# Down products of a feed-forward block copied by ScalarE and added to the residual by an accumulating transfer, with three operand turns moved back to TensorE

## The reference

```
h = h + jnp.concatenate([oa, ob, oc, od], axis=-1) @ w_out[i]
y = _rms(h, norm_ffn_g[i])
h = h + (jax.nn.silu(y @ w_gate[i]) * (y @ w_up[i])) @ w_down[i]
y = _rms(h, norm_ple_g[i])
h = h + jax.nn.sigmoid(y @ w_ple_gate[i]) * (p[i] @ w_ple_proj[i])
return _rms(h, final_norm_g)
```

## Time and profile before

| | us |
|---|---|
| median of three runs | 2066.68 (2064.77 to 2067.17) |
| the profiled execution, its own time | 2066.98 |
| its span, first to last instruction | 2065.2 |
| PE busy in the span | 2039.0 |
| DVE busy | 1583.2 |
| ACT busy | 1041.8 |
| POOL busy | 175.6 |
| mean granted clock of TensorE, share of full speed | 0.996 |

### The profile page before, as it was taken

How to read it: one execution, slowest core, us unless ns; L and a number is a source line. 1 busy time by engine, 2 the same in 40 slices (tenths; PEclk the granted TensorE clock), 3 DMA queues, 4 the chain that set the end, 5 groups by cost and what they waited for, 6 DMA issues and landing times.

```text
span 2065.2 us, 24990 instructions
## 1 busy us (share of the span) xinstructions
PE 2039.0 (99%) x10231; PEld 1733.1 (84%) x10231; DVE 1583.2 (77%) x1511; ACT 1041.8 (50%) x979; POOL 175.6 (9%) x354
## 2 busy tenths in 40 slices
PE   9999999999999999999999998999999999999998
PEld 8888888888888888888999987888888888888787
DVE  6576565665688888856889868989888889888565
ACT  6444444544455555645344445554555545455543
POOL 2000110010000000023000012111110011110100
PEclk9999999999999999999999999999999999999999
DMA  8655556555465655666655566765666665566561
GB/s 251 215 183 177 180 171 190 172 189 194 166 224 204 224 204 183 204 233 205 206 186 165 178 220 199 234 213 194 198 214 224 214 212 194 194 232 224 173 207 58
DMA packets 234689, 408.33 MB, mean 198 GB/s; under 512 B 16226, under 2 KB 61530, under 8 KB 234320
## 3 DMA queue, kind: packets, MB, share of 16 engines
q1 hardware_dynamic: 221344, 387.64, 56.7%
q0 software_dynamic: 12480, 17.98, 3.1%
q10 hardware_dynamic: 752, 1.12, 0.2%
HBM read 394.62 MB, written 2.12 MB: 192 GB/s over the span
## 4 chain that ended last, share of the span: by engine, by line
PE 87%; DVE 9%; ACT 1%; DMA 1%; issue 1%; POOL 1%; ACTq 0%; SPq 0%; DVEq 0%
PE psA L750 20%; PE psA L752 20%; PE psA L751 20%; PE psA L957 6%; PE psB L750 5%; PE psB L751 5%; PE psB L752 5%; PE psA L961 3%; DVE lo L1759 3%; DVE CA L2083 1%; POOL squares in X L679 1%; DVE raw L1776 1%; DMA squares in X<-squares in X 1%; DVE lo in Y L1759 1%; ACT hi L1274 0%
## 5 line engine op out<-in xcount | busy, mean ns | idle before, releaser
L1759 DVE TENSOR_TENSOR lo<-raw,hi 128x2048 fp32r<-128x2048 f32 (+2 forms) x364 | 822.3, 2268 | 254.1 <-ACT hi L1274 253.0
L1274 ACT ACTIVATE hi<-raw 128x2048 fp32r<-128x2048 f32 (+2 forms) x364 | 688.9, 1899 | 469.8 <-PE psA L752 303.9
L750 PE MATMUL psA<-hi,XHL 128*128 128x512 f32 x1008 | 394.1, 391 | 0.8 <-DVE XHL L1860 0.8
L752 PE MATMUL psA<-hi,XHL 128*128 128x512 f32 x1008 | 391.0, 388 | 0.0
L751 PE MATMUL psA<-lo,XHL 128*128 128x512 f32 (+1 forms) x872 | 338.0, 388 | 0.0
L750 PE MATMUL psA<-hi,YHL 128*128 128x512 f32 x624 | 244.3, 391 | 0.0
L752 PE MATMUL psA<-hi,YHL 128*128 128x512 f32 x624 | 243.3, 390 | 0.0
L750 PEld LDWEIGHTS psA<-hi,XHL 128*128 128x128 f32 x1008 | 189.6, 188 | 40.0 <-issue 1.5
L752 PEld LDWEIGHTS psA<-hi,XHL 128*128 128x128 f32 x1008 | 189.4, 188 | 39.1
L751 PE MATMUL psA<-lo,YHL 128*128 128x512 f32 x536 | 209.1, 390 | 0.0
L751 PEld LDWEIGHTS psA<-lo,XHL 128*128 128x128 f32 x872 | 164.2, 188 | 32.6
(11 more groups left out here) (441 smaller groups left out, 3003.7 us busy)
## 6 DMA issues: line engine op xcount, KB each, us to landing
raw<-in_w_in_dram SPq DMA_DIRECT2D x149, 1024.0 KB, 5.1
raw<-in_w_up_dram SPq DMA_DIRECT2D x35, 1024.0 KB, 5.2
raw<-in_w_gate_dram SPq DMA_DIRECT2D x35, 1024.0 KB, 5.2
raw<-in_w_out_dram SPq DMA_DIRECT2D x32, 1024.0 KB, 5.1
raw<-in_w_down_dram SPq DMA_DIRECT2D x32, 1024.0 KB, 5.2
raw<-in_w_ple_gate_dram SPq DMA_DIRECT2D x14, 1024.0 KB, 5.1
raw<-in_w_branch_dram SPq DMA_DIRECT2D x13, 1024.0 KB, 5.1
raw in Y<-in_w_down_dram SPq DMA_DIRECT2D x12, 1024.0 KB, 5.1
```

The costliest lines, as they stand in the source:

```text
L750: e.matmul(dst, A2[0], B2[0], start=first, stop=False, skip_group_check=True)
L752: return e.matmul(dst, A2[1], B2[0], start=False, stop=last, skip_group_check=True)
L1274: e.activation(hi[u % H][:, 0:m], raw[slot][:, 0:m], ACT.Copy).then_inc(hi_made, 1)
L1759: e.tensor_tensor(lo[slot][:, 0:m], raw[slot][:, 0:m], hi[u % H][:, 0:m].bitcast(F32), ALU.subtract).then_inc(lo_made, 1)
```

## The change

The residual sums of the first nine down parts (36 products) leave VectorE. ScalarE copies each from PSUM into a new tile TD (which takes the place of HB), and GpSimd issues a DMA that adds TD to 512 columns of X (`accum_op=ALU.add`). The copy waits until the sum before it has landed (`x_added`), and GpSimd's DMA waits for the copy. The four products of the last down part stay with VectorE. The hidden block is now written over CG, its squares are moved into THF, and so two waits are new: ScalarE's copy of unit x waits for the squares of the hidden block before, and its first tanh waits until the moved block has been read. The moved block is read at unit BEGIN[j + 1] + 2 (6 for j = 0), and before at + 8. Three turns of X (FIRST 2, SECOND 2, THIRD 0; 24 transposes) go from the second way to the first, and the units at which TensorE turns X are set anew. The iterations of the row scale of the feed-forward norm go from VectorE to GpSimd, 14 steps with a wait behind each. GpSimd's queue in the feed-forward part holds, for each turn: eight DMAs of the move, the sum of down product 0, eight DMAs of the move, the sums of products 1, 2 and 3.

```diff
-        self.by_act = kind != "T2" and name[0] in ("narrow", "qi", "v", "gate", "v2", "scc", "proj", "ple")
+        self.by_act = kind != "T2" and (name[0] in ("narrow", "qi", "v", "gate", "v2", "scc", "proj", "ple")
+                                        or name[0] == "down" and name[1] < 4 * LAST_TURN)
...
-            HB = sb("HB", [128, 2, 512], F32, p4)
+            TD = sb("TD", [128, 1024], F32, p4)
...
+        def emptied(name):
+
+            g = named[name]
+            return bank_act if g.by_act else bank_dve, g.freed
...
-        MOVES = (0, 1, 2, FIRST, FIRST + 1, FIRST + 2, SECOND, SECOND + 2) + tuple(HIDDEN + j for j in range(10)) + (THIRD,)
+        MOVES = (0, 1, 2, FIRST, FIRST + 1, SECOND) + tuple(HIDDEN + j for j in range(10))
...
-        TURN1 = {OUT + 18: 3}
-        TURN2 = {OUT2 + 10: 1, OUT2 + 18: 3}
+        TURN1 = {OUT + 6 + 4 * f: f for f in (2, 3)}
+        TURN2 = {OUT2 + 6 + 4 * f: f for f in (1, 2, 3)}
...
-        TURN3 = {named["down", LAST_DOWN + f].last + 5 - f: f for f in (1, 2, 3)}
-        MOVEDX = {OUT + 8: (FIRST, 0, 16), OUT + 12: (FIRST, 1, 16), OUT + 15: (FIRST, 2, 16),
-                  OUT2 + 8: (SECOND, 0, 32), OUT2 + 15: (SECOND, 2, 32), named["down", LAST_DOWN].last + 5: (THIRD, 0, 48)}
+        TURN3 = {named["down", LAST_DOWN + f].last + 2: f for f in range(4)}
+        MOVEDX = {OUT + 8: (FIRST, 0, 16), OUT + 12: (FIRST, 1, 16), OUT2 + 8: (SECOND, 0, 32)}
...
-        MOVEDH = {BEGIN[j + 1] + 8: j for j in range(10)}
+        MOVEDH = {BEGIN[j + 1] + (2 if j else 6): j for j in range(10)}
...
+            def ffn_root():
+
+                y, w = rr_, w2_
+                e.wait_ge(root_begun, 1)
+                for _ in range(3):
+                    finish(e.tensor_tensor(w, y, y, ALU.mult))
+                    finish(e.tensor_tensor(w, w, v2, ALU.mult))
+                    finish(e.tensor_scalar(w, w, -0.5, 1.5, ALU.mult, ALU.add))
+                    finish(e.tensor_tensor(y, w, y, ALU.mult))
+                finish(e.tensor_scalar(hr2, y, 0.5, None, ALU.mult))
+                e.tensor_tensor(r2h, hr2, y, ALU.mult).then_inc(ffn_scales, 1)
...
-            for j in range(10):
-                move(HIDDEN + j, turning(block_of(j)), flat(HB[:, :, :]))
-            move_x(THIRD, 0)
+            ffn_root()
+            def add_down(n):
+
+                f = n % 4
+                e.wait_ge(*emptied(("down", n)))
+                e.dma_start(cols(f), TD[:, :].rearrange("p (t n) -> p t n", t=2), accum_op=ALU.add).then_inc(x_added, 16)
+
+            move(HIDDEN, turning(block_of(0)), THF[:, :])
+            for j in range(9):
+                n, squares = HIDDEN + j + 1, turning(block_of(j + 1))
+                move(n, squares, THF[:, :], (0, 1))
+                add_down(4 * j)
+                move(n, squares, THF[:, :], (2, 3))
+                for f in (1, 2, 3):
+                    add_down(4 * j + f)
...
                     elif j:
-                        e.wait_ge(*up(j - 1, "hidden"))
+                        e.wait_ge(squares_turned, squared(HIDDEN + j - 1))
                     e.activation(gates_sum[:, 512:1024], quarter(g, "C"), ACT.Copy).then_inc(sum_copied, 1)
...
                     e.wait_ge(ffn_scales, 1)
+                    if j:
+                        e.wait_ge(flip_low, HIDDEN + j)
                     e.activation(THF[:, 512:1024], CG2, ACT.Tanh, scale=hr2[:, 1:2])
...
-                elif name == "down" and n >= LAST_DOWN:
+                elif name == "down" and n < LAST_DOWN:
+                    if n:
+                        e.wait_ge(x_added, 16 * n)
+                    take(TD[:, :])
+                elif name == "down":
                     e.wait_ge(bank_dve, g.freed)
                     squares(n - LAST_DOWN, X, ss4, ss4_made)
...
-                elif name == "down":
+                elif name == "down" and n >= LAST_DOWN:
                     f = n % 4
+                    e.wait_ge(x_added, 16 * LAST_DOWN)
                     e.wait_ge(unit_done, g.last + 1)
                     e.wait_ge(bank_dve, g.freed - 1)
                     e.tensor_tensor(cols(f), cols(f), ps.rearrange("p (t n) -> p t n", t=2), ALU.add).then_inc(bank_dve, 1)
-                    if n == LAST_DOWN:
-                        e.wait_ge(bank_dve, g.freed)
-                        turn_x_squares(f)
```

More of the change, by code:

```diff
@@ L410, in build_hybrid @@
         bank_act, bank_dve, crossed = sem("bank_act"), sem("bank_dve"), sem("crossed")
-        act_step, dve_step = sem("act_step"), sem("dve_step")
+        act_step, dve_step, pool_step, root_begun = [sem(n) for n in ("act_step", "dve_step", "pool_step", "root_begun")]
         x_landed = [sem(f"x_landed{i}") for i in range(4)]
@@ L447, in build_hybrid @@
         squares_turned, squares_moved = sem("squares_turned"), [sem(f"squares_moved{i}") for i in range(2)]
+        x_added = sem("x_added")
         sum_copied, gate_made, up_made, gates_ready = [sem(n) for n in ("sum_copied", "gate_made", "up_made", "gates_ready")]
@@ L672, in gpsimd_program, with finish, move @@
         def gpsimd_program(e):
-            def move(n, squares, dst):
+            steps = [0]
+            def finish(x):
+                steps[0] += 1
+                x.then_inc(pool_step, 1)
+                e.wait_ge(pool_step, steps[0])
+            def ffn_root():
[8 more added lines that the diff above has]
+                e.tensor_tensor(r2h, hr2, y, ALU.mult).then_inc(ffn_scales, 1)
+            def move(n, squares, dst, quads=range(4)):
                 to = dst.rearrange("p (q n) -> p q n", q=4)
                 e.wait_ge(squares_turned, squared(n))
-                for q in range(4):
+                for q in quads:
                     for r in range(4):
@@ L716, in gpsimd_program @@
                     e.dma_start(FW[:, :], rows(A["final_norm_w"], 2048)).then_inc(fw_landed, 16)
-            for f in range(3):
+            for f in range(2):
                 move_x(FIRST, f)
@@ L729, in gpsimd_program @@
                             ).then_inc(mixers_landed, 16)
-            for f in (0, 2):
-                move_x(SECOND, f)
+            move_x(SECOND, 0)
             e.wait_ge(unit_done, done(("out2", 3)))
@@ L815, in bank_free @@
                 elif name == "down" and n == 2:
-                    e.wait_ge(bank_dve, freed(("down", 0)))
+                    e.wait_ge(*emptied(("down", 0)))
                 elif name == "down" and n == 3:
@@ L822, in bank_free @@
                     if f == 0:
-                        e.wait_ge(bank_dve, freed(("down", n - 1)))
+                        e.wait_ge(*emptied(("down", n - 1)))
                     elif f == 1:
@@ L830, in bank_free @@
                     else:
-                        e.wait_ge(bank_dve, freed(("down", n - 3)))
+                        e.wait_ge(*emptied(("down", n - 3)))
                 elif name == "down" and n == LAST_DOWN:
-                    e.wait_ge(bank_dve, freed(("down", n - 1)))
+                    e.wait_ge(*emptied(("down", n - 1)))
                 elif name == "down" and n == LAST_DOWN + 1:
@@ L862, in mixed_free @@
                     else:
-                        e.wait_ge(bank_dve, freed(("down", 4 * (j - 2) + 1)))
+                        e.wait_ge(*emptied(("down", 4 * (j - 2) + 1)))
                 elif name == "D" and j == 1:
@@ L866, in mixed_free @@
                 elif name == "D" and j:
-                    e.wait_ge(bank_dve, freed(("down", 4 * (j - 2) + 2)))
+                    e.wait_ge(*emptied(("down", 4 * (j - 2) + 2)))
                 elif name == "B":
@@ L1230, in side @@
                     e.wait_ge(flip_low, HIDDEN + j)
[L1231 removed]
+                    flip(lambda t, k: CG[:, 512 * t + 128 * k:512 * t + 128 * k + 128], 1)
                 if u in TURN3:
[L1233 removed]
+                    e.wait_ge(*emptied(("down", LAST_DOWN + TURN3[u])))
                     e.wait_ge(pt_made, 1)
@@ L1285, in high @@
                 e.wait_ge(flip_turned, turned(n))
-                if n in (FIRST + 3, SECOND + 3, THIRD + 3):
-                    e.wait_ge(flip_low, n)
+                if n in (FIRST + 2, FIRST + 3, SECOND + 3):
+                    e.wait_ge(flip_low, {FIRST + 2: FIRST + 2, FIRST + 3: FIRST + 1, SECOND + 3: SECOND + 1}[n])
                 if isinstance(scale, float):
@@ L1297, in high_moved @@
                 e.wait_ge(*landed_square(n))
-                if n == FIRST + 2:
-                    e.wait_ge(flip_low, n)
                 if isinstance(scale, list):
```

28 lines of the change are left out of this document (13 added, 15 removed).

## The result

The changed kernel takes 2091.1 us (median of four runs, 2088.7 to 2092.5) against 2066.9 for the kernel before, run beside it: ratio 1.0119, interval 1.0107 to 1.0132. It is 1.2% slower. The forecast was 2057.7 us and its range ended at 2080. The profiled execution of the changed kernel took 2092.4 us, span 2090.6.

The account below looks back on a forecast made before the run. TensorE was taken as the bound, busy 2039 of 2065.2 us. Terms -0.3 - 4.5 - 0.9 - 3.2 = -8.9 from 2066.98, less 0.3 for the median, gave 2057.7 us; range 2053 to 2080.

Parts of the forecast that it names:

- "Cost nothing" for the copies and accumulating transfers: Nine feed-forward turns: ScalarE's copies hide in its idle time and transfers land in time, so 0 us.
- L: Time from issue to landing of an accumulating transfer: taken as 4.7 us, free up to 5.3, then 27 us per us.
- slow landing: Rival, chance 0.22: transfers in the feed-forward turns land after 5.3 us; 2077 us at 6, up to 2090 to 2105.
- Turns on TensorE, +0.9 each: Three turns of X moved back to TensorE: each costs 0.89 us, +2.7 us together, counted at their places.
- First output projection, -0.3: Earlier addition of the fourth product removes TensorE's 1.2 us wait for the scales; the added turn costs 0.9.
- Second, -4.5: Second output projection: addition 4.2 us earlier, no halved clock (1.8), losses of 0.9 and 0.6; -4.5 us, added turn contained.
- Row scale: Feed-forward norm on GpSimd: 14 steps at 0.5 us, 7 us, free up to 18; VectorE's relief saves 0.9 at a split.
- Last turn of X, -3.2: End of the feed-forward part: the 2.4 us wait and its 1.7 us of halved clock go, the added turn costs 0.9.
- VectorE's relief wins nothing: Feed-forward part: 36 additions leaving VectorE, about 44 us, win nothing, since TensorE never waits for VectorE there.
- The signs named for a wrong forecast: ScalarE idle before TD copies, nine TensorE waits, first tanh waiting for GpSimd, TensorE busy time up over 3 us.
- The slower side: Whole kernel measured above 2070.8 us, chance 0.26; nearly all of slow landing is in it.
- the likeliest case: Whole kernel as forecast, between 2054 and 2062 us, chance 0.55.

Follow-up runs that it names:

- plain_write: Changed kernel with transfers that overwrite X instead of adding, so the feed-forward sums are left out: 2060.7 us, ratio 0.9977.
- three_sums: Changed kernel with products 0, 1 and 2 of each turn summed by transfer and product 3 on VectorE: 2069.9 us, ratio 1.0017.
- scale_back: sums_vector with the row scale moved back from GpSimd to VectorE: 2061.1 us, ratio 0.9976.
- turn_later: sums_vector with the second block of the last X turned one unit later: 2058.8 us, ratio 0.9963.
- sums_vector: Changed kernel with the 36 sums back on VectorE and no accumulating transfer, all else as changed: 2060.6 us, ratio 0.9975.
- every_other: Changed kernel with only products 0 and 2 of each turn summed by transfer, 1 and 3 on VectorE: 2061.1 us, ratio 0.9977.

## Why the prediction was wrong

**The step that failed is "Cost nothing" for the copies and accumulating transfers**, where 31.0 us were measured, and in it the value of L. I took 4.7 us between rows for loads. Measured: 5.9 in the median. A plain transfer of the same bytes takes 4.6, about what I had taken for the accumulating one; the latter takes 0.5 us more to issue and twice the time on the engines. I had written that each packet has two reads and gave them no time of their own. The Trainium skill (DMA: Bandwidth & Descriptors, Anatomy of one DMA — SWDGE (gpsimd) path) would have had 3.2 us for a plain one by its fit; the shortest of the 36 plain ones took 3.2, but the median of 4.6, beside weight loads, is 1.4 longer, and for the accumulate's 5.9 the fit is further off.

**The threshold and the price of TensorE's idle time were right.** By the prediction a landing is free up to 5.3 us, and each of three landings in a turn costs what it has beyond that. The table gives, for each turn, by how much its first three landings (from issue to landing, as in the view of the tile TD) exceed 3 x 5.3 = 15.9 us, how long TensorE was idle, and what the turn cost by unit ends, in us:

```
turn                    1     2     3     4     5     6     7     8     9    sum
landings less 15.9     1.3   0.8   6.4   0.7   1.1   7.8   1.3   0.8   1.3   21.6
TensorE idle           1.3   1.0   4.9   0.9   1.5   7.7   1.5   1.1   1.5   21.2
cost                   2.0   1.6   8.2   1.5   2.1   9.8   2.1   1.7   2.0   31.0
```

So the chain that I had named carries the long turns too; only the third is off by more than 0.4. What no step spoke of is the other 9.8 us: 4.4 at half clock, which the rival "slow landing" had named, and 0.6 a turn beside the idle time. Nor did any step say that a landing isn't one number: those of the seven ordinary turns would cost 7.4 us of idle time by this, the rest is in two turns, where a load starts just behind a sum. That 3 x (5.9 - 5.3) = 1.8 us comes near the cost of an ordinary turn is luck: the median of 5.9 takes in the fourth sums, which hold up nobody, and the cost takes in those 0.6. plain_write with 4.6 us cost nothing. And the threshold is one of two: the split behind the copy is late as well, 3.0 us of the third turn's idle time and every wait of TensorE in the nine turns of three_sums.

**Turns on TensorE, +0.9 each: right.** At the added turn of the last X the unit ends move from -5.08 to -4.21 in scale_back, where nothing else happens.

**First output projection, -0.3: right** (-0.4; the wait for the scales is gone). **Second, -4.5: right** (-4.2; waits 6.1 to 0.5, clock 0.86 to 1.00, and 1.7 us of wait for the low part of the fourth piece, 0.8 before; the replay had 0.9 and 0.6 of losses).

**Row scale: right that it costs nothing, wrong in its length and its gain.** Of the 14 steps on GpSimd in the changed kernel, and what waits for them:

```profile
1271.81 2.16 POOL L692 TENSOR_TENSOR SM<-SM 128x2 f32<-128x2 f32 x1 [15.94 <-DVE SM L2317]
...
1276.27 0.19 POOL L694 TENSOR_SCALAR SM<-SM 128x2 f32<-128x2 f32 x1
...
1283.50 2.31 POOL L696 TENSOR_SCALAR SM<-SM 128x2 f32<-128x2 f32 x1
...
1286.18 0.72 ACT L1601 ACTIVATE THF<-CG,SM 128x512 f32<-128x512 f32 x1 [4.01 <-POOL SM L697]
```

The steps take 14.3 us, 1.0 each, twice what I took and under the 1.3 up to which I had called them free; five take 2.1 to 2.3, the length of a VectorE subtraction, one 0.5, the others 0.2. The Trainium skill (SBUF — State Buffer, Who interferes with whom) says that of a VectorE instruction with two SBUF inputs and a GpSimd instruction that reads SBUF one waits for the other's end; the trace agrees, with 2.2 us against 0.2. The gain at S1 is 0.25, not 0.9: a wait of 0.7 us for a split stays, 0.9 before. I had taken it for granted that VectorE's relief reaches that wait in full. The last row above is ScalarE's first tanh: it did wait 4.0 us for the scales, which was one of the signs of a wrong forecast, but the cover named for it held, and TensorE waits for nothing behind it.

**Last turn of X, -3.2: the mechanism right, the schedule of the change not read closely enough.** In the changed kernel it is -1.3. The 2.4 us wait and its halved clock go, but a new one of 1.6 us comes at the second turn, which stands one unit behind the first and needs its low part; ScalarE has a pair of squares in front of the high part:

```profile
1958.16 0.60 ACT L1348 ACTIVATE psB<-X 128x512 f32<-128x512 f32 x1 [3.49 <-DVE X L2432]
...
1959.55 1.55 ACT L1329 ACTIVATE XHL<-psB,VC 128x256 fp32r<-128x256 f32 x4
```

I had followed the third and the fourth turn and not the second. turn_later takes the wait away and gains the 3.2.

**VectorE's relief wins nothing: right** (sums_vector and every_other are the same).

**The signs named for a wrong forecast came as named:** ScalarE idle ahead of the copies into TD behind a DMA, TensorE waiting nine times in the units behind them, ScalarE's first tanh behind GpSimd (at no cost), and TensorE's busy time up by 12 us, four times the 3 that I had named.

**The chances.** The slower side had 0.26, the likeliest case 0.55. The trace had no row for the landing, the margin was 0.6 us in a chain of three with a price of 27 us per us, and there was a named reason for a longer landing. The range should have reached the 2090 to 2105 that the rival itself gave. (The terms of the sum give 2057.8, not 2057.7; nothing hangs on it.)

## What to carry to other kernels

A transfer that takes over an addition is free only while it lands before its buffer is wanted again. With one buffer and several in a row the lateness adds up, and everything queued behind the copy on its engine is late with it, splits and bank releases alike: look at both. Put such transfers at every other product, or give them two buffers (the latter was not tried), before counting the relief of an engine that holds nobody up. A landing time under load is a spread and not a number: look at what the other queue starts just ahead of the transfer and just behind it.

## What the runs showed of the hardware

- An accumulating transfer of 512 KB from SBUF to SBUF: 5.0 to 9.9 us to landing, 5.9 in the median, 3.2 us of all 16 DMA engines, 1.23 us of GpSimd for the issue. The same without accumulating: 3.2 to 7.4, 4.6 in the median, 1.5 and 0.73. The first runs as 256 packets of 2 KB, the second as 128 of 4 KB.
- Half of it, with the other half beside it: 5.3 us. Cutting the transfer in two shortened the landing by 0.6 us.
- Small moves of 32 KB behind or beside such transfers land in 3.9 us instead of 1.7. The list of DMA issues of the changed kernel:

```profile
THF<-raw in Y POOLq DMA_DIRECT2D x160, 32.0 KB, 3.9
```

- The four sums with a weight load issued within 1 us behind them landed in 6.8 to 9.5 us, against 5.0 to 6.3; held off, they landed in 5.0 to 5.9.
- In each of the two long turns the granted clock was 0.50 for 6.8 us (0.76 over 14 us), which is 1.2 of 2.4 GHz. It fell within a stop of TensorE, of 3.0 us in the third turn and of 6.9 us in the sixth. In the seven ordinary turns, with one stop of 0.9 to 1.5 us each, it stayed at 1.00.

Open: how much of the accumulating transfer's landing is the adding and how much its smaller packets; why sum 8 was issued late and sum 20 landed late, which starts the two long turns; and what the nine turns would cost with all 36 sums and no load just behind a sum.
